# Padded full-array matmuls and per-turn turning of B in place of 32-row and 32-column groups in the S5 stage

## The reference, cut to what matters

```python
def even_layer(x, ...):
    hn = rmsnorm(x, norm_g)
    q, k, v, u, z_a, z_b = split(hn @ w_in)          # 1024 columns each
    o_a = chunked_relpos_attention(q, k, v, rel_bias) * silu(z_a)
    y = gelu(s5_ssm(u, lam_re, lam_im, log_dt, b_re, b_im, c_re, c_im, d_skip))
    o_b = y * sigmoid(y @ w_glu + b_glu) * silu(z_b)
    return x + concatenate([o_a, o_b]) @ w_out
```

## Time and profile before

| what | value |
|---|---|
| median of 3 runs | 3165.55 us |
| lowest and highest | 3162.47, 3168.78 us |
| the profiled execution's own time | 3165.55 us |
| its span in the profile | 3163.6 us |
| granted TensorE clock, mean | 0.973 |

### The profile page before, as it was taken

The page is one execution under the profiler, slowest core; times in us unless marked ns, Lnnn a source line. Parts: engine busy times, 40 slices in busy tenths (PEclk is TensorE's granted clock), DMA queues, the critical chain, the costliest instruction groups (busy, mean ns, idle before and its releaser), DMA issues.

```text
span 3163.6 us, 42503 instructions
## 1 busy us (share of the span) xinstructions
PE 2988.6 (94%) x18260; PEld 2123.6 (67%) x18260; DVE 1516.2 (48%) x1799; ACT 837.7 (26%) x926; POOL 274.5 (9%) x245
## 2 busy tenths in 40 slices
PE   8999999999999999999999999879999999999998
PEld 6777777899977743333333333358758878997886
DVE  4455544764556522322222222276886554444655
ACT  3352222544434311101101100010001334443343
POOL 2042111000000000000000000036530000000000
PEclk9999988999999999999999999989999999999899
DMA  7543221346565589999999999944444475887453
GB/s 246 153 136 106 75 61 56 120 134 186 179 228 186 181 347 424 425 425 425 425 425 425 425 425 425 419 138 141 141 139 127 146 179 126 180 190 160 100 164 136
DMA packets 215215, 722.08 MB, mean 228 GB/s; under 512 B 16170, under 2 KB 18634, under 8 KB 164716
## 3 DMA queue, kind: packets, MB, share of 16 engines
q1 hardware_dynamic: 210716, 702.22, 63.4%
q0 software_dynamic: 3216, 14.97, 1.3%
q10 hardware_dynamic: 1088, 2.10, 0.2%
HBM read 717.13 MB, written 2.10 MB: 227 GB/s over the span
## 4 chain that ended last, share of the span: by engine, by line
PE 73%; DMA 12%; DVE 10%; ACT 4%; issue 1%; POOL 0%; DVEq 0%; ACTq 0%
PE psum L137 72%; DMA t<-in_w_up 12%; DVE t L283 7%; ACT t L254 2%; DVE t L294 1%; PE psum L143 1%; ACT t L256 1%; DVE t L298 0%; DVE t L306 0%; ACT L254 0%; ACT L256 0%; POOL t L328 0%; DMA t<-in_x 0%; DVE t L275 0%; DVEq L77 0%
## 5 line engine op out<-in xcount | busy, mean ns | idle before, releaser
L137 PE MATMUL psum<-t,t 128*128 128x256 f32 (+10 forms) x17230 | 2899.9, 380 | 125.2 <-DVE t L283 70.0
L137 PEld LDWEIGHTS psum<-t,t 128*128 128x128 f32 (+4 forms) x17230 | 2038.6, 175 | 949.6 <-issue 584.4
L283 DVE TENSOR_TENSOR t<-t,t 128x1024 fp32r<-128x1024 f32 (+6 forms) x642 | 779.2, 1214 | 501.9 <-ACT t L254 469.3
L254 ACT ACTIVATE t<-t 128x1024 fp32r<-128x1024 f32 (+8 forms) x521 | 528.5, 1014 | 900.6 <-PE psum L137 655.7
L283 DVE TENSOR_TENSOR t<-t,psum 128x1024 f32<-128x1024 f32 (+3 forms) x265 | 246.4, 930 | 739.8 <-PE psum L137 440.0
L254 ACT ACTIVATE t<-psum 128x1024 f32<-128x1024 f32 (+5 forms) x278 | 213.5, 768 | 1382.8 <-PE psum L137 1284.3
L328 POOL TENSOR_TENSOR t<-t,t 128x1024 f32<-128x1024 f32 (+9 forms) x125 | 216.5, 1732 | 512.8 <-DVE t L283 223.6
L283 DVE TENSOR_TENSOR t<-psum,t 128x1024 f32<-128x1024 f32 (+5 forms) x125 | 100.3, 802 | 147.0 <-PE psum L137 99.5
L143 PE MATMUL psum<-t,t 128*128 128x128 f32 (+1 forms) x518 | 80.1, 293 | 29.4 <-DVE t L294 18.0
L143 PEld LDWEIGHTS psum<-t,t 128*128 128x128 f32 (+1 forms) x518 | 60.5, 148 | 66.0 <-issue 39.5
L83 POOL DMA_DIRECT2D t<-in_s_lr x1 | 0.6, 574 | 1185.2 <-DVE t L306 1185.2
(11 more groups left out here) (65 smaller groups left out, 243.6 us busy)
## 6 DMA issues: line engine op xcount, KB each, us to landing
t<-in_w_gate SPq DMA_DIRECT2D x128, 1024.0 KB, 16.9
t<-in_w_up SPq DMA_DIRECT2D x128, 1024.0 KB, 18.4
t<-in_w_down SPq DMA_DIRECT2D x128, 1024.0 KB, 17.5
t<-in_w_in SPq DMA_DIRECT2D x160, 512.0 KB, 4.2
t<-in_w_in_odd SPq DMA_DIRECT2D x128, 512.0 KB, 5.4
t<-in_w_in_even SPq DMA_DIRECT2D x96, 512.0 KB, 3.8
t<-in_w_out SPq DMA_DIRECT2D x32, 512.0 KB, 4.6
t<-in_w_pg SPq DMA_DIRECT2D x32, 512.0 KB, 4.1
```

Of the source, the lines that this page charges most:

```text
L137: ins = self.e.matmul(o, l, r, start=start, stop=stop, skip_group_check=True)
L254: self.put(self.e.activation(o, i, f, scale=scale), event)
L283: self.put(self.e.tensor_tensor(o, a, b, op), event)
```

## The change

The packed tiles go. `b_times_u` and `y_of` use the whole array: a turn's b and c are laid out in pads of 128 partitions by 4 blocks of 128 columns, in which block q holds its 32 channels at columns 32q and zeros elsewhere (a pad is 640 wide, so that one access pattern with a stride of 160 reaches the four places). The pads are for one turn: VectorE fills `pads[0:2]` with b for turn j + 1 ahead of the sum and difference of turn j, and `pads[2:4]` with c for turn j after the scans, 4 copies of 64x64 each. b is turned in each turn by 8 transposes of 128x128 (`turn_b(j + 1)`, after `y_of(j - 1)`), and copied to one tile `BT` in each turn (`turned_b(j + 1)`, after the scans). The results of `b_times_u` go to the regions that `pe.take` gives. All 16 pieces of `ev.u` come before `turn_b(0)`, and they take PSUM regions 1 and 2. `scratch` and `far` lie over b's and c's inputs and `Bb[2]`, and GpSimd waits for `s5.setup`, the last operation of VectorE's set-up, in place of `s5.cos`.

```diff
@@ -512,24 +512,22 @@
         vve = tm(1024)
         yT = uT
         s5_at = top[0]
-        bre, bim, cre, cim = [at(top[0] + 512 * k, 512).rearrange("p (i c) -> p i c", i=32) for k in range(4)]
-        BT = alloc(2048).rearrange("p (j z c) -> p j z c", j=8, z=2)
-        far = [alloc(256).rearrange("p (i t) -> p i t", i=32) for _ in range(2)]
-        scratch = alloc(1024)
-        spun = psum[:, 2048:4096].rearrange("p (q z t) -> p q z t", q=4, z=2)
+        bre_at = top[0]
+        bre, bim, cre, cim = [alloc(512).rearrange("p (i c) -> p i c", i=32) for _ in range(4)]
+        Bb = [alloc(512).rearrange("p (i c) -> p i c", i=32) for _ in range(3)]
         lr, li, ld = alloc(32), alloc(32), alloc(32)
         dt, mag, ang, k2, sn, cs_, are, aim, den, cr, ci_, tA, tB, tC = [alloc(32) for _ in range(14)]
-        cpad = [alloc(1024).rearrange("p (i x) -> p i x", i=32) for _ in range(2)]
-        mm_at = top[0] + 4096
+        pads = [alloc(640) for _ in range(4)]
+        BT = alloc(1024).rearrange("p (z i c) -> p z i c", z=2, i=4)
         phases, MM = [[[alloc(1024).rearrange("p (i t) -> p i t", i=4) for _ in range(2)] for _ in range(2)]
                       for _ in range(2)]
         Z1, Z2 = [alloc(1024).rearrange("p (i t) -> p i t", i=4) for _ in range(2)]
-        Bb = [at(mm_at + 512 * k, 512).rearrange("p (i c) -> p i c", i=32) for k in range(3)]
-        bpad = [at(mm_at + 2048 + 1024 * k, 1024).rearrange("p (i x) -> p i x", i=32) for k in range(2)]
         gz = alloc(256)
         squares = [at(xT_at + 4096 + 1024 * k, 1024) for k in range(2)]
         spread_row = at(xT_at + 6144, 256)
         few = [at(6144 + 1024 * k, 1024).rearrange("p (i t) -> p i t", i=32) for k in range(2)]
+        far = [at(bre_at + 3072 + 256 * k, 256).rearrange("p (i t) -> p i t", i=32) for k in range(2)]
+        scratch = at(bre_at, 1024)
         bw = at(8192, 4096).rearrange("p (h x) -> p h x", h=16)
         top[0] = s5_at
         oT = fm(16)
@@ -1127,10 +1125,11 @@
                         yield
 
             def even():
-                first = native_b("ev.u", hTe, "w_in_even_2", 3072, 1024, (0, 1))
+                first = native_b("ev.u", hTe, "w_in_even_2", 3072, 1024, (1, 2))
                 for k in range(8):
                     pe.wait_ge(("ev.hT", 2 * k + 1))
                     some(first, 1)
+                some(first, 8)
                 rest = chain(native_b("ev.q", hTe, "w_in_even_2", 0, 1024, (0, 1)),
                              native_b("ev.k", hTe, "w_in_even_2", 1024, 1024, (0, 1)),
                              native_a("ev.v", hTe, "w_in_even_2", 2048, 1024, (0, 1)),
@@ -1138,44 +1137,39 @@
                              native_b("ev.zb", hTe, "w_in_even_2", 5120, 1024, (0, 1)),
                              native_b("s5.glu", yT, "w_glu_2", 0, 1024, (0, 1)))
 
-                def turn_b(g):
-                    ps = pe.take("s5.bt", g, of=(2, 3))
-                    pe.wait_ge(("s5.padb",))
-                    for i in range(4):
-                        for z in range(2):
-                            pe.tr(ps[:, 256 * i + 128 * z:256 * i + 128 * z + 128],
-                                  bpad[z][:, 16 * g + 4 * i:16 * g + 4 * i + 4, :].rearrange("p i x -> p (i x)"),
-                                  event=("s5.bt", g) if i == 3 and z else None)
-
-                def b_times_u(j):
-                    for k in range(2):
-                        pe.take("s5.bu", j, k, of=(2, 3))
-                    pe.wait_ge(("s5.btc", j // 4), ("ev.u.c", j // 4))
+                def turn_b(j):
+                    ps = pe.take("s5.bt", j, of=(2, 3))
+                    pe.wait_ge(("s5.padb", j))
                     for z in range(2):
                         for q in range(4):
-                            rows = slice(32 * q, 32 * q + 32)
-                            pe.mm(spun[:, q, z, :], BT[rows, j, z, :], uT[rows, j, :], True, True,
-                                  event=("s5.bu", j) if z and q == 3 else None)
+                            pe.tr(ps[:, 512 * z + 128 * q:512 * z + 128 * q + 128], pads[z][:, 128 * q:128 * q + 128],
+                                  event=("s5.bt", j) if z and q == 3 else None)
+
+                def b_times_u(j):
+                    br_, bi_ = [pe.take("s5.bu", j, z, of=(2, 3)).rearrange("p (i t) -> p i t", i=4) for z in range(2)]
+                    pe.wait_ge(("s5.btc", j), ("ev.u.c", j // 4))
+                    for q in range(4):
+                        pe.mm(br_[:, q, :], BT[:, 0, q, :], uT[:, j, :], True, True)
+                        pe.mm(bi_[:, q, :], BT[:, 1, q, :], uT[:, j, :], True, True,
+                              event=("s5.bu", j) if q == 3 else None)
 
                 def y_of(j):
                     ps = pe.take("s5.y", j, of=(2, 3))
                     M1, M2 = MM[j % 2]
-                    pe.wait_ge(("s5.m", j), ("s5.padc",))
-                    for z, m in enumerate((M1, M2)):
-                        for q in range(4):
-                            pe.mm(ps[32 * q:32 * q + 32, 0:256], cpad[z][:, 4 * j + q, :], m[:, q, :], z == 0, z == 1,
-                                  event=("s5.y", j) if z and q == 3 else None)
-
-                some(first, 1)
-                for g in range(2):
-                    turn_b(g)
-                some(first, 2)
+                    pe.wait_ge(("s5.m", j), ("s5.padc", j))
+                    for q in range(4):
+                        pe.mm(ps[:, 0:256], pads[2][:, 128 * q:128 * q + 128], M1[:, q, :], q == 0, False)
+                        pe.mm(ps[:, 0:256], pads[3][:, 128 * q:128 * q + 128], M2[:, q, :], False, q == 3,
+                              event=("s5.y", j) if q == 3 else None)
+
+                turn_b(0)
                 b_times_u(0)
-                some(first, 5)
                 for j in range(8):
                     some(rest, 2)
                     if j:
                         y_of(j - 1)
+                    if j < 7:
+                        turn_b(j + 1)
                     some(rest, 4)
                     if j < 7:
                         b_times_u(j + 1)
@@ -2100,23 +2094,23 @@
                 v.tt(Bb[1], bim, crb, ALU.mult)
                 v.tt(Bb[2], bre, cib, ALU.mult)
                 v.tt(Bb[1], Bb[1], Bb[2], ALU.add)
-                for z in range(2):
-                    for hf in range(2):
-                        pa = slice(64 * hf, 64 * hf + 64)
-                        v.copy(bpad[z][pa, :, 16 * hf:16 * hf + 16], Bb[z][pa])
-                v.names(("s5.padb",))
-                for hf in range(2):
-                    pa = slice(64 * hf, 64 * hf + 64)
-                    v.copy(cpad[0][pa, :, 16 * hf:16 * hf + 16], cre[pa])
-                    v.ts(cpad[1][pa, :, 16 * hf:16 * hf + 16], cim[pa], -1.0, None, ALU.mult)
-                v.names(("s5.padc",))
+                v.ts(cim, cim, -1.0, None, ALU.mult, event=("s5.setup",))
 
             def s5():
-                def turned_b(g):
-                    v.wait_ge(("s5.bt", g))
-                    v.copy(BT[:, 4 * g:4 * g + 4], v.bank("s5.bt", g).rearrange("p (j z c) -> p j z c", j=4, z=2),
-                           event=("s5.btc", g))
-                    v.free("s5.bt", g)
+                def pad(j, zs, srcs, event):
+                    for z, src in zip(zs, srcs):
+                        d = z.rearrange("p (i x) -> p i x", i=4)
+                        for hf in range(2):
+                            pa = slice(64 * hf, 64 * hf + 64)
+                            v.copy(d[pa, :, 16 * hf:16 * hf + 16], src[pa, 4 * j:4 * j + 4, :])
+                    v.names(event)
+
+                def turned_b(j):
+                    v.wait_ge(("s5.bt", j))
+                    if j:
+                        v.wait_ge(("s5.bu", j - 1))
+                    v.copy(BT, v.bank("s5.bt", j).rearrange("p (z i c) -> p z i c", z=2, i=4), event=("s5.btc", j))
+                    v.free("s5.bt", j)
 
                 def gelu(j):
                     y1 = yT[:, j, :]
@@ -2133,12 +2127,12 @@
                     v.wait_ge(("s5.tanh", j))
                     v.stt(y1, gz, 1.0, y1, ALU.add, ALU.mult, event=("s5.yT",) if j == 7 else None)
 
-                for g in range(2):
-                    turned_b(g)
+                pad(0, pads[0:2], Bb[0:2], ("s5.padb", 0))
+                turned_b(0)
                 for j in range(8):
                     CC, SS = phases[j % 2]
                     M1, M2 = MM[j % 2]
-                    br_, bi_ = [spun[:, :, z, :] for z in range(2)]
+                    br_, bi_ = [v.bank("s5.bu", j, z).rearrange("p (i t) -> p i t", i=4) for z in range(2)]
                     v.wait_ge(("s5.bu", j), ("s5.phases", j))
                     if j > 1:
                         v.wait_ge(("s5.y", j - 2))
@@ -2150,6 +2144,9 @@
                     v.free("s5.bu", j, 1)
                     if j == 7:
                         gate_z("ev.za", za, 0)
+                    if j < 7:
```

(10 more changed lines are left out.)

## The result

The changed kernel takes 3215.69 us in the median (3209.98 to 3226.59, 4 runs), the kernel before 3167.16 us (3162.47 to 3170.32, 4 runs). The ratio is 1.016, with a 95% interval from 1.0138 to 1.0182: 48.5 us slower by the medians, against 3216 us forecast. The profiled execution has a span of 3213.3 us, 49.7 us more than before.

What follows compares the result with a forecast made beforehand. TensorE was taken to bound the changed stage, with no wait to take away. The terms 37.8 + 5.2 + 1.6 + 4.4 + 1.7 = +50.7 us on 3165.55 us gave 3216 us, range 3211 to 3221 us (chance 0.52).

Steps and rivals of the forecast that it cites:

- Matmuls on the whole array: In TensorE's loop, eight b_times_u and eight y_of become 8 full matmuls each: 55.6 us in place of 17.8, +37.8 us.
- the price of the packed groups: Eight packed groups each of b_times_u and y_of on TensorE: 1.15 and 1.08 us a group, 17.8 us in all.
- Transposes: On TensorE, eight turn_b of 8 transposes at 0.109 us each: 7.0 us in place of 1.75, +5.2 us.
- Wait ahead of `b_times_u(0)`: At the loop's start TensorE waits for VectorE's copy out of PSUM with nothing queued: 1.6 us (1.4 to 1.8).
- Wait ahead of `turn_b(1)`: In the first turn TensorE waits for VectorE's four pad(1) copies, blocked by GpSimd's products: 4.4 us (0 to 7).
- later start of the phases: GpSimd begins only at s5.setup, before turn 0; on its own this costs nothing or 1 us.
- Lower clock behind it: TensorE runs below full clock after the 4.4 us gap ahead of turn_b(1): 1.7 us (0 to 2.5).
- Sum: Over the whole execution, 37.8 + 5.2 + 1.6 + 4.4 + 1.7 = +50.7 us on 3165.55 us, giving 3216 us.
- rival 1: At pad(1), small copies slip between GpSimd's products at 0.2 us, no blocking: 44.6 us remain, 3210 us; chance 0.2.
- rival 2: In the steady loop VectorE becomes the bound, turns of 37 to 38 us: 3226 us; chance 0.15.
- Rival 3: Not slower: without array-shape changes TensorE's pieces run faster; hidden gain or a later wait 0.05, not slower by 0.2% 0.02.
- Rival 4: Zero blocks or overlapping accumulations make the new groups cheaper, 2.5 us in place of 3.5: 3200 us; chance 0.08.

Runs made afterwards that it cites:

- y_packed: Changed kernel with y_of alone back on packed groups of 32 columns: median 3205.7 us, ratio 1.0102 to the kernel before.
- bu_packed: Changed kernel with b_times_u alone back on packed groups of 32 rows: median 3203.2 us, ratio 1.0102 to the kernel before.
- all_but_turns_act: Changed kernel with y_of and b_times_u packed, the old order of ev.u, and pad copies on ScalarE: median 3179.9 us, ratio 1.0026 to before.
- u_split: Changed kernel with the old order of ev.u pieces and its old PSUM regions at the loop's start: median 3212.6 us, ratio 1.0125 to before.
- phases1_late: Changed kernel in which GpSimd makes the phases of turn 1 only once pad(1) is done: median 3220.9 us, ratio 1.0150 to before.
- own_scratch: Changed kernel with GpSimd's old start at s5.cos, its first short table made in an early-free buffer: median 3212.5 us, ratio 1.0124 to before.
- pads_twice: Changed kernel with each pad copied twice, 16 small copies a turn in place of 8: median 3223.8 us, ratio 1.0160 to before.
- pads_on_act: Changed kernel with all pad copies on ScalarE in place of VectorE: median 3221.1 us, ratio 1.0145 to before.
- all_but_turns: Changed kernel with y_of and b_times_u packed and the old order of ev.u, pads and transposes left: median 3193.3 us, ratio 1.0064 to before.
- own_scratch_split: Changed kernel with GpSimd's old start at s5.cos and the old order of ev.u: median 3214.7 us, ratio 1.0130 to before.

## Why the prediction was right

The forecast was 3216 us, the time 3215.7 us. The terms of the sum were right in kind and place. Two were too large, the matmuls by 2.0 us and the wait at `turn_b(1)` by 2.05, and what lay outside the sum made up for them.

- **Matmuls on the whole array**, +37.8 us forecast. The turns of y_packed and bu_packed give 18.4 + 17.4 = 35.8 us. A full matmul took 0.432 us rather than 0.434: a steady turn is 80 of them and 0.87 us of transposes, (35.41 - 0.87)/80. The step that was mis-sized is the price of the packed groups: read as 1.15 and 1.08 us from the busy time by shape, they are 3.45 - 2.18 = 1.27 (rows) and 3.45 - 2.30 = 1.15 us (columns). The turn of before bears this out: 64 x 0.432 + 1.27 + 1.15 = 30.07 us, against 30.10 between two starts of VectorE's products.
- **Transposes**, +5.2 us forecast, 5.3 us left over in all_but_turns_act.
- **Wait ahead of `b_times_u(0)`**, 1.6 us forecast, 1.41 us in the profile; gone in u_split.
- **Wait ahead of `turn_b(1)`**, 4.4 us (0 to 7) forecast, 2.35 us measured. The mechanism was the one named (phases1_late, own_scratch), the size of the blocking was not. I gave each small copy a whole product of GpSimd; only every second one waits, four copies taking 4.04 us and not 6. The Trainium skill, SBUF — State Buffer, section "SBUF: two separate sides", has the loser of the port that VectorE and GpSimd share blocked for the whole instruction of the other. That agrees with the copies of 1.77 and 1.78 us; but a short one passed between them while a product was under way by its row. I also called the later start of the phases free on its own (0 to 1 us). With one thing changed at a time that is so in the kernel before (0.99 us), and not so in the changed one, where it is a condition of this wait. (The working left out the negation of 0.6 us when it shifted the phases to 2169.6 us; nothing hangs on it, as VectorE's turn 0 waited for TensorE there.)
- **Lower clock behind it**, +1.7 us forecast, 1.70 us measured. That it came was luck: in bu_packed a longer wait had none.
- **Sum**: 35.8 + 5.3 + 1.4 + 2.35 + 1.7 = 46.6 us, against 46.7 us of the stretch and 50.7 us forecast. That the total was met to a microsecond is luck. The stretch came out 4.0 us below the sum. The profile has 3.0 us more outside it (5.1 behind, where untouched code had more of the lower clock, 2.1 less ahead), and the medians differ by 48.5 us, 2.2 less than the sum. The median of before then was 1.6 us above the 3165.55 that the forecast started from. Single runs of the changed kernel range over 16.6 us.

The rivals: blocking exists (rival 1 falls), though every second copy does slip through at the 0.2 us that rival 1 gave to all. VectorE is not the bound in the changed kernel (rival 2: pads_twice, pads_on_act), but its chain of 33 us was near enough to become it once the matmuls were packed. Its length was forecast at 34.0 us and is 32.98 in all_but_turns. Rival 3, a gain by fewer changes of the array's shape, falls by its size: those changes are worth at most the 0.3 to 0.4 us by which a packed group exceeds the 0.86 us of two full matmuls, 5.6 us over the loop, all inside the 35.8. Rival 4 falls: at 2.5 us a group, the two of a turn would leave it at some 33.5 us, and it is 35.41.

## What to carry to other kernels

Where one engine fills a stage and the others wait for it, the price of a change is the work that it adds to that engine, counted in instructions by shape: that was 41 of 47 us here. Take the price of a small group from the length of a turn, not from its busy time. Work that is hidden behind such a stage is not free to keep when the stage gets shorter: the pads cost 4 us in the changed kernel, all of it in the first turn, and 14 us in the version with packed matmuls (321.5 - 307.1), more than half of it in the later turns, so three edits that gave 41 us one by one gave 25.6 together. And look for blocking between engines at the first turn, where buffers and tables come late, rather than in the steady loop.

## What the runs showed of the hardware that was not expected

- Beside a run of GpSimd products of 1.9 us, VectorE's 64x64 copies inside SBUF go in pairs, one blocked (1.77 us) and one at its own speed (0.19 us); eight copies took 7.9 us in a steady turn of pads_twice, and four 3.35 us in the changed kernel. Eight scans of 0.72 us each took 14.35 us beside six products.
- Whether TensorE falls to the lower clock behind a wait is not settled by its length: 2.35 us (changed kernel) cost 1.70 us and 2.23 us (y_packed) 1.65 us, while 2.59 us (bu_packed) and 1.97 us (u_split) cost nothing. The granted clock of the 4 us behind the wait is 0.58, 0.59, 1.00 and 1.00 in this order. What ran ahead of the waits was the same work in the first two, all but one packed group of it in bu_packed, and the same in another order in u_split. The same 3.79 us ahead of `ev.u` were followed by 9 pieces in 34.2 us or, in own_scratch_split, in 31.35 us. What decides this stays open.
